# Attention's second preparation moved from the back stage into the end of the front stage of a fused decoder kernel

## The reference, cut to what matters

```python
def _rms(x, g):
    y = xf * lax.rsqrt(jnp.mean(xf * xf, axis=-1, keepdims=True) + NORM_EPS)
    return (y * g.astype(jnp.float32)).astype(x.dtype)
...
out = jnp.concatenate([x1 * cos - x2 * sin, x2 * cos + x1 * sin, xf[..., rd:]], axis=-1)   # _rope, rd = 32 of 128
```

## Time and profile before

| | us |
|---|---|
| median of 3 runs | 1884.52 |
| lowest and highest | 1884.0, 1885.48 |
| profiled execution, its own time | 1886.33 |
| its span, first to last instruction | 1884.7 |
| mean granted clock of TensorE | 0.976 |
| busy time of PE, DVE, ACT, POOL | 1782.6, 978.1, 601.3, 413.1 |

### The profile page before, as it was taken

One profiled execution on the slowest core, in us unless ns is written; L12 is line 12 of the kernel. 1 busy time (PEld: TensorE's weight loads), 2 busy tenths in 40 slices (PEclk: granted clock), 3 DMA queues, 4 the chain that ended last, 5 costly groups with the idle time before them and its releaser, 6 DMA issues. The chain is left out here.

```text
span 1884.7 us, 26517 instructions
## 1 busy us (share of the span) xinstructions
PE 1782.6 (95%) x9417; PEld 1377.3 (73%) x9417; DVE 978.1 (52%) x2277; ACT 601.3 (32%) x1275; POOL 413.1 (22%) x646
## 2 busy tenths in 40 slices
PE   6999999999999998999999998999989579999999
PEld 5666888777788876887876566887767456777887
DVE  5513643233377665221632567888876665775111
ACT  3111332111022112210321346787734345554010
POOL 4301221000134352000342001211005365330000
PEclk9999999999899999999999999999999789999999
DMA  6334333444355467321322121334333764332331
GB/s 214 126 115 125 113 113 108 147 160 125 120 166 180 149 194 276 133 90 44 116 64 79 45 74 63 114 97 143 125 119 98 252 218 149 116 99 89 109 115 47
DMA packets 134349, 236.97 MB, mean 126 GB/s; under 512 B 28486, under 2 KB 60774, under 8 KB 134218
## 3 DMA queue, kind: packets, MB, share of 16 engines
q1 hardware_dynamic: 110506, 171.96, 28.2%
q0 software_dynamic: 17328, 56.24, 9.4%
q10 hardware_dynamic: 6384, 7.08, 1.1%
HBM read 169.05 MB, written 66.17 MB: 125 GB/s over the span
## 5 line engine op out<-in xcount | busy, mean ns | idle before, releaser
L1212 PE MATMUL layer_acc<-layer_w_hi,layer_xT_hi 128*128 128x512 f32 x640 | 262.5, 410 | 0.2 <-PE all_banks L1360 0.2
L1214 PE MATMUL layer_acc<-layer_w_hi,layer_xT_lo 128*128 128x512 f32 x640 | 253.7, 396 | 0.0
L1213 PE MATMUL layer_acc<-layer_w_lo,layer_xT_hi 128*128 128x512 f32 x640 | 253.3, 396 | 0.0
L2773 PE MATMUL front_acc<-front_w_hi,front_xT_hi 128*128 128x512 f32 x520 | 219.8, 423 | 16.0 <-DVE front_st L3253 6.4
L2775 PE MATMUL front_acc<-front_w_hi,front_xT_lo 128*128 128x512 f32 x520 | 207.9, 400 | 0.0
L2774 PE MATMUL front_acc<-front_w_lo,front_xT_hi 128*128 128x512 f32 x520 | 207.5, 399 | 0.0
L1212 PEld LDWEIGHTS layer_acc<-layer_w_hi,layer_xT_hi 128*128 128x128 f32 x640 | 122.1, 191 | 30.7 <-issue 5.9
L1213 PEld LDWEIGHTS layer_acc<-layer_w_lo,layer_xT_hi 128*128 128x128 f32 x640 | 121.6, 190 | 26.7 <-issue 2.6
L1214 PEld LDWEIGHTS layer_acc<-layer_w_hi,layer_xT_lo 128*128 128x128 f32 x640 | 121.2, 189 | 27.0
L2773 PEld LDWEIGHTS front_acc<-front_w_hi,front_xT_hi 128*128 128x128 f32 x520 | 99.6, 192 | 48.8 <-issue 11.8
L3099 ACT ACTIVATE front_index_rows<-odd_bias,front_candidate 128x1024 bf16<-128x1024 f32 (+3 forms) x128 | 124.9, 981 | 8.6 <-DVEq L3453 5.0
(11 more groups left out here) (675 smaller groups left out, 3592.8 us busy)
## 6 DMA issues: line engine op xcount, KB each, us to landing
all_w<-in_w_even POOLq DMA_DIRECT2D x80, 256.0 KB, 3.7
h_even<-layer_st SPq DMA_DIRECT2D x79, 256.0 KB, 2.1
all_w<-in_w_odd POOLq DMA_DIRECT2D x61, 256.0 KB, 3.5
h_odd<-front_st SPq DMA_DIRECT2D x55, 256.0 KB, 2.0
layer_scratch<-h_even SPq DMA_DIRECT2D x46, 256.0 KB, 3.2
all_scratch<-in_w_mem SPq DMA_DIRECT2D x32, 256.0 KB, 4.0
all_scratch<-h_even SPq DMA_DIRECT2D x32, 256.0 KB, 3.7
all_scratch<-x SPq DMA_DIRECT2D x14, 512.0 KB, 3.6
```

Source lines behind the costliest of these rows:

```text
L1212: T.matmul(out[0:rows, :], xh[:, kk, to], wh[:, r, :], start=(kk == 0), stop=False)
L1213: T.matmul(out[0:rows, :], xh[:, kk, to], wl[:, r, :], start=False, stop=False)
L1214: ins = T.matmul(out[0:rows, :], xl[:, kk, to], wh[:, r, :], start=False, stop=(kk == KC - 1))
L2773: T.matmul(out[0:rows, :], xh[:, k, to], wh[:, r, :], start=(k == 0), stop=False, skip_group_check=True)
```

## The change

Tile 1 is prepared in the front stage too, in a third buffer `c.qk[2]` (columns 2560 to 3840 of the scratch), where ACT's squares were written so far; these go to free columns of the index rows. SP issues a third load of 640 KB in slot 62. ACT's order becomes squares 0, squares 1, scaling 0, squares 2, scaling 1, scaling 2 in slots 63 to 68; POOL's becomes roots 0, roots 1, weighing 0, rotation 0 and weighing 1, rotation 1 in slots 64 to 68, then roots 2 and weighing 2 in slot 69 and rotation 2 in slot 70. In the back stage all of tile 1's preparation but the transposes and the store of its keys goes, TURN[2] becomes 1, and ACT's squares for p = 3, which are written over tile 1's buffer, wait for the transposes and the store of tile 1.

```diff
-        FIRST_TILES = (0, TILES)
+        FIRST_TILES = (0, TILES, 1)
+        squares_out = Q[:, 2640:2640 + QK]
...
             def heads_ready():
-                for _ in range(3):
+                for _ in range(2):
                     yield
                 head_rstds(0)
                 yield
...
                 weighted(1)
                 yield
                 rotated(1)
+                yield
+                head_rstds(2)
+                weighted(2)
+                yield
+                rotated(2)
...
-                        ins = A(S[0:rows, 2560 + HD * h:2688 + HD * h], c.qk[u][0:rows, e], ACT.Square, accum_out=c.qk_ssq[u][0:rows, h:h + 1])
+                        ins = A(squares_out[0:rows, e], c.qk[u][0:rows, e], ACT.Square, accum_out=c.qk_ssq[u][0:rows, h:h + 1])
...
+                yield
+                squared(0)
+                yield
+                squared(1)
+                yield
+                scaled(0)
+                yield
+                squared(2)
+                yield
+                scaled(1)
+                yield
+                scaled(2)
+                yield
...
-    TURN = {p: 4 if p == 2 else 6 for p in START}
+    TURN = {p: 1 if p == 2 else 6 for p in START}
...
+        qk_of = lambda p: c.qk[2 if p == 2 else p % 2]
...
         def wait_rotated(eng, p):
-            if p == 2:
-                eng.wait_ge(rq2, 1)
-            else:
+            if p > 2:
                 eng.wait_ge(rq, p - 2)
...
             def preps():
-                load_qk(2)
                 load_k(2)
                 load_value(0)
                 load_value(1)
+                load_value(2)
...
                         if at == 0:
-                            pool.wait_ge(red, p - 1)
+                            pool.wait_ge(red, p - 2)
                             link(G.tensor_tensor(ssq[u][0:rows, :], ssq[u][0:rows, :], c.half[0:rows, 0:H10], ALU.pow))
-                            if p == 2:
-                                pool.sem_inc(rsd, 1)
-                                continue
...
             def first_squares(p):
                 u, rows = p % 2, rows_in(PREP[p])
-                act.wait_ge(qk_in[u], 16 * (p // 2))
-                if p > 2:
-                    act.wait_ge(red, p - 2)
-                A(sq[0:rows, :], qk[u][0:rows, :], ACT.Square).then_inc(squ, 1)
+                act.wait_ge(qk_in[u], 16 * ((p - 1) // 2))
+                if p == 3:
+                    act.wait_ge(qtr, 3)
+                    act.wait_ge(kst[0], 16)
+                else:
+                    act.wait_ge(red, p - 3)
+                A(sq[0:rows, :], qk_of(p)[0:rows, :], ACT.Square).then_inc(squ, 1)
...
-                first_squares(2)
...
-                        if step == 2:
-                            dve.wait_ge(rsd, 1)
-                            link(V.tensor_tensor(y, y, bc(ssq[u][0:rows, :], 2, HD), ALU.mult))
-                            for lo, hi, j, n in ((0, QH * HD, 0, QH), (QH * HD, QK, 1, KVH)):
-                                part = heads(qk[u][0:rows, lo:hi], n)
-                                link(V.tensor_tensor(part, part, bc(gam[0:rows, j, :], 1, n), ALU.mult))
-                        if step == 3:
-                            rotate(V, link, y, HD // 8, rt[:, PREP[p]], tmp, rows, H10)
-                            dve.sem_inc(rq2, 1)
...
-        c.qk = [S[:, H * HD * u:H * HD * (u + 1)] for u in range(2)]
+        c.qk = [S[:, H * HD * u:H * HD * (u + 1)] for u in range(3)]
```

More of the change, by code:

```diff
@@ L2385, in layer1_front @@
         xhi, whi = s.sem("first_xT_upper"), s.sem("first_weights_upper")
-        qk_in, qk_par, hsq, hrs, hsc, hgd, hrq, b_out, kp_in = (s.sem("qk_in", 2), s.sem("qk_gammas_rope_in"), *(s.sem(n) for n in (
+        qk_in, qk_par, hsq, hrs, hsc, hgd, hrq, b_out, kp_in = (s.sem("qk_in", 3), s.sem("qk_gammas_rope_in"), *(s.sem(n) for n in (
             "head_squares", "head_rstd_made", "head_scaled", "head_weighted", "head_rotated", "bias_out", "first_k_pages_in")))
         H10, QK = QH + KVH, (QH + KVH) * HD
-        FIRST_TILES = (0, TILES)
+        FIRST_TILES = (0, TILES, 1)
+        squares_out = Q[:, 2640:2640 + QK]
         BOTH = slice(SEQ, TOK + SMP)
@@ L2567, in loads_qk @@
                 yield
-                for u, t in enumerate(FIRST_TILES):
+                for u, t in enumerate(FIRST_TILES[:2]):
                     to = o[9][0, 0, cols_in(t)].rearrange("t h d -> t (h d)") if t < TILES else o[12][0].rearrange("b t h d -> (b t) (h d)")
@@ L3197, in head_squares, with squared, scaled @@
             def head_squares():
[L3198 to L3201, removed]
+                def squared(u):
+                    rows = rows_in(FIRST_TILES[u])
                     act.wait_ge(qk_in[u], 16)
                     if u:
-                        act.wait_ge(hsq, 1)
+                        act.wait_ge(hsq, u)
                     for h in range(H10):
                         e = slice(HD * h, HD * h + HD)
-                        ins = A(S[0:rows, 2560 + HD * h:2688 + HD * h], c.qk[u][0:rows, e], ACT.Square, accum_out=c.qk_ssq[u][0:rows, h:h + 1])
+                        ins = A(squares_out[0:rows, e], c.qk[u][0:rows, e], ACT.Square, accum_out=c.qk_ssq[u][0:rows, h:h + 1])
                     ins.then_inc(hsq, 1)
-                    yield
-                for u, t in enumerate(FIRST_TILES):
-                    rows = rows_in(t)
+                def scaled(u):
+                    rows = rows_in(FIRST_TILES[u])
                     act.wait_ge(hrs, u + 1)
@@ L3700, in layer1_back @@
         sq = X[:, 2560:3840]
-        qk, gam, tmp, ssq = c.qk, c.qk_gam, c.qk_tmp, c.qk_ssq
+        gam, tmp, ssq = c.qk_gam, c.qk_tmp, c.qk_ssq
+        qk_of = lambda p: c.qk[2 if p == 2 else p % 2]
         WH, WL = G[:, 0:OUT_CHUNKS * D], G[:, OUT_CHUNKS * D:2 * OUT_CHUNKS * D]
@@ L3785, in load_qk @@
                     sp.wait_ge(kst[u], 16 * (p // 2 - 1))
-                sp.dma_start(qk[u][0:rows_in(t), :], c.h_odd[cols_in(t), 0:QK]).then_inc(qk_in[u], 16)
+                sp.dma_start(qk_of(p)[0:rows_in(t), :], c.h_odd[cols_in(t), 0:QK]).then_inc(qk_in[u], 16)
                 load_value(p)
@@ L3957, in preps @@
                         rows, u = rows_in(PREP[p]), p % 2
-                        y = heads(qk[u][0:rows, :], H10)
+                        if p == 2:
+                            continue
+                        y = heads(qk_of(p)[0:rows, :], H10)
                         at = step - 1
                         if at == 0:
-                            pool.wait_ge(red, p - 1)
+                            pool.wait_ge(red, p - 2)
                             link(G.tensor_tensor(ssq[u][0:rows, :], ssq[u][0:rows, :], c.half[0:rows, 0:H10], ALU.pow))
-                            if p == 2:
-                                pool.sem_inc(rsd, 1)
-                                continue
                             link(G.tensor_tensor(y, y, bc(ssq[u][0:rows, :], 2, HD), ALU.mult))
-                        if p == 2:
-                            continue
                         if at == 1:
                             for lo, hi, j, n in ((0, QH * HD, 0, QH), (QH * HD, QK, 1, KVH)):
-                                part = heads(qk[u][0:rows, lo:hi], n)
+                                part = heads(qk_of(p)[0:rows, lo:hi], n)
                                 link(G.tensor_tensor(part, part, bc(gam[0:rows, j, :], 1, n), ALU.mult))
@@ L4040, in preps @@
                             at = P * (4 * j + h)
-                            ins = T.transpose(bankQ[:, rows * h:rows * h + rows], qk[u][0:rows, at:at + P], c.ident[0:rows, 0:rows])
+                            ins = T.transpose(bankQ[:, rows * h:rows * h + rows], qk_of(p)[0:rows, at:at + P], c.ident[0:rows, 0:rows])
                         ins.then_inc(qtr, 1)
@@ L4260, in preps @@
                         rows = rows_in(t)
-                        if step == 0:
+                        if step == 0 and p > 2:
                             first_squares(p)
@@ L4359, in preps @@
                         rows = rows_in(t)
-                        y = heads(qk[u][0:rows, :], H10)
-                        if step == 1:
-                            dve.wait_ge(squ, p - 1)
+                        if step == 1 and p > 2:
+                            dve.wait_ge(squ, p - 2)
                             link(V.tensor_reduce(ssq[u][0:rows, :], heads(sq[0:rows, :], H10), AX.X, ALU.add))
                             V.tensor_scalar(ssq[u][0:rows, :], ssq[u][0:rows, :], 1.0 / HD, EPS, ALU.mult, ALU.add).then_inc(red, 1)
-                        if p > 2:
-                            continue
-                        if step == 2:
-                            dve.wait_ge(rsd, 1)
-                            link(V.tensor_tensor(y, y, bc(ssq[u][0:rows, :], 2, HD), ALU.mult))
-                            for lo, hi, j, n in ((0, QH * HD, 0, QH), (QH * HD, QK, 1, KVH)):
```

(7 more changed lines are left out.)

4 lines of the change are left out of this document (1 added, 3 removed).

## The result

The changed kernel takes 1896.66 us (median of 5 runs, 1893.36 to 1904.48), the kernel before 1884.52 beside it: ratio 1.0066, 95% interval 1.0054 to 1.0078. It is 12.1 us slower; 1892.8 was forecast, in a range of 1886.5 to 1897.5.

What follows compares the result with a forecast made beforehand. PE was taken as busy nearly throughout, so only its idle stretches or a stage's end it does not set count. 1886.3 + 11.3 (front) − 3.0 (back) = 1894.6, less 1.8 for the median: 1892.8 us, range 1886.5 to 1897.5.

Steps and rivals of the forecast that it cites:

- Steps 1 and 2: Front, slots 63 to 68: ACT's added squares make Tanh 64 2.0 us late; DVE's idle leaves 1.5 at the sample scalings.
- Step 3: Front, slot 68: ACT waits for POOL's third roots, ready 11.0 us after the sample scalings end.
- Step 4: Front: Tanh 68, behind the waiting ACT, comes 14.3 us later; PE idles 8.3 us ahead of unit 70.
- Step 5: End of front: after 3.0 us of slack, the ACT and DVE chain and the front's end move 11.3 us later.
- POOL's last work: End of front: POOL's weighing and rotation of tile 1 end before the front does, hidden by 6 us.
- 1.4 + 1.6 = 3.0 us gained: Back: 1.4 us from removing the 640 KB load, 1.6 from moving tile 1's transposes out of slots 5 to 7.
- So it is kept: Back: the 3.0 us gain lasts because POOL's chain of tile 2 starts that much sooner.
- low bound was 1.5 gained: Back: smallest expected gain, 1.5 us, if SP's added work and tile 3's load eat half.
- rival C: Front loses 15 to 17 us through slow POOL pieces, low clock and late key pages; 1897.5 us, chance 0.13.
- low bound of 9.5: Front: smallest expected loss, 9.5 us, with POOL undisturbed throughout and weighing taking 3.7 us.
- Rival A: Front: third roots are ready when ACT asks, so the front hides the work; 1881.5 us, chance 0.09.
- B: Back gives up to 9.1 us through prompt pages, full clock and the DVE stall removed; 1886.7 us, chance 0.08.

Runs made afterwards that it cites:

- e1: The changed kernel with POOL making tile 1's third roots ahead of weighing tile 8, not behind its rotation; 1889.47 us, ratio 1.0035 to the kernel before.
- e2: The changed kernel with ACT's third scalings two slots later, in slot 70 instead of 68; 1892.94 us, ratio 1.0050 to the kernel before.
- e4: The changed kernel's back with the front of the kernel before, which only loads tile 1; 1886.07 us, ratio 1.0010 to the kernel before.
- e5: The changed kernel with POOL issuing the key pages of units 6 and 7 only after unit 4 is transposed; 1896.15 us, ratio 1.0062.
- e6: e1 with SP sending pages of units 4 and 5 ahead of bias rows, tile 2's load and two value stores; 1886.62 us, ratio 1.0009.
- e3: The changed kernel's front with the back of the kernel before, so tile 1 is loaded and prepared twice; 1896.27 us, ratio 1.0069.
- e9: e8 with SP's bias row loads moved between the pages of units 4 and 5; 1881.50 us, ratio 0.9994 to the kernel before.
- e7: The kernel before with e6's order of SP's queue; 1884.71 us, ratio 0.9997 to the kernel before.
- e8: e6 with tile 1's rotation moved from POOL in the front to DVE in slot 1 of the back; 1883.89 us, ratio 1.0002.

## Why the prediction was right, and where it was not

**Steps 1 and 2, the first slots.** Right at first: Tanh 64 stands 6.87 us behind the first row of the stretch against 4.85, +2.0. Then DVE's slack took more than I thought. The sample scalings begin 23.20 us from that row against 22.58, +0.6 where I had +1.5.

**Step 3, ACT's wait for the third roots.** Forecast 11.0 us from the end of the sample scalings to the roots. It was 11.1 (1442.78 to 1453.88), of which ACT idled 10.65. The pieces were 5.17 for weighing, 3.04 for the rotation, 2.6 for the roots: the three of my sum. The rotation ran at 0.52 us an operation, undisturbed, with DVE at a stand, as forecast. e1 removed this wait and took 10.3 us off the front.

**Step 4.** PE idle 8.41 us ahead of unit 70, forecast 8.3. Tanh 68 is later by 13.5, forecast 14.3; the 0.9 of step 2 is the difference.

**Step 5.** DVE's product of unit 68 moved from 30.36 to 40.97 us from the first row, +10.6, forecast +11.3. Then +11.67 at Tanh 69, at the sample half and at Tanh 71. Between, DVE's first small operation of the ties took 1.25 us beside POOL's weighing of tile 1, where it had taken 0.51, and the product behind it 1.65 for 1.33. So the front's 11.67 against 11.3 is 0.7 less at one place and 1.1 more at another. I had called POOL's last work hidden. No wait shows it, but DVE ran slower next to it.

**The back, the step that failed: "1.4 + 1.6 = 3.0 us gained".** Its first term, 1.4 us for pages that land earlier, was nothing. The page was issued 0.6 us earlier and took 0.65 longer; in the other four kernels without the load and with SP's order as it was (e1, e2, e4, e5) unit 4 came at 19.6 to 21.2 us from the back's start, against 19.8 in before. What set it was the rest of SP's queue, tile 2's load, bias rows and value stores, all still ahead of it: with those behind it (e6) unit 4 came 5.2 us sooner. I had priced the removed load by its bytes and not asked what else stood in the same queue, nor whether those bytes were moved while the page was awaited: they were moved ahead of its issue. The second term, 1.6 us for three slots, showed in after as 1.4 at unit 5, 1.1 at unit 8 and 0.8 at tile 2's transposes, and in e1 and e2, from the back's start, not at all; its 0.65 for slot 5 was about right (0.5 to 0.9 at like clocks). "So it is kept" was wrong: slot 22 came 0.7 later than before, since PE worked longer at the low clock from 83 us on. What sets where that clock rises (86.9 us in before, 88.6 in after, 88.8 in e4, but 87.6 in e5 with POOL's pages held) no run varied alone, so this stays open. The four backs of after's code (after, e1, e2, e4) are 0.7 to 2.0 us longer than the two of before's (before, e3), and by e4's time the back costs 1.6: a loss, where the low bound was 1.5 gained.

**Sum.** 11.67 + 0.73 = 12.4 against 11.3 − 3.0 = 8.3: 4.1 us more, all but 0.4 of it the back's. The sign and the size of the loss are the front's, and its 0.4 is the sum of two misses that partly cancel. 1896.66 lies above the forecast's own upper bound of 1896.3; it is in the stated range only because that reached into rival C, whose front of 15 to 17 us did not come. (The front's low bound of 9.5 is a slip: 11.3 less the 1.5 us between a weighing of 5.2 and one of 3.7 is 9.8.) Rival A fell with ACT's wait; B's 9.1 us was nowhere, but e9 shows that the back holds 2.8 us once SP's order lets it.

## What to carry to other kernels

Before an engine gets a wait, write down what its producer must finish first and what stands behind the waiting instruction: roots of 2.6 us cost 11.7, as they stood behind another tile's work on POOL and ahead of a Tanh on ACT, and moving one line brought 10.3 back in the front, of which the gap took 1.8. A removed load gives its bytes' time only if the late transfer waited for those bytes; look at what else stands in the queue ahead of it, and at what ends just before the wait does. When work goes to the end of a stage, compare the time from each engine's last instruction to the next stage, and not its last Tanh alone.

## What the hardware did that I had not expected

The next stage begins 6.0 us after POOL's last instruction when POOL is late: 6.04 us in e1, 6.03 in e2 and e6, though POOL ends 0.5 us ahead of the beginning of Tanh 71 in e1 and e6 and 1.1 behind it in e2, where the back otherwise starts 3.75 us from the beginning of ACT's last Tanh (before, after, e3, e4, e5, e7, e8, e9). In before POOL had ended 13.3 us ahead, in after 12.3, so nothing showed. e8 took the last rotation, 4.7 us, off POOL, and the gap went from 5.52 to 3.75. Which part of the 6.0 us is POOL's own and which the barrier's no row tells.
